# Fifteen instead of eight convolution strips made beside the projections, and a convolution block with wider rings

## Chip, core and metric

One core of one Trainium2 chip runs the whole program as one launch. The metric is the device time of that launch in microseconds, median over runs. PE is TensorE (PEld its weight loads), DVE VectorE, ACT ScalarE, POOL GpSimd, SP SyncE, which only issues transfers and waits here.

## What is computed

One layer of a hybrid decoder, for 528 prompt tokens (16 learned ones and 512 given) and 8 x 4 sample tokens, 560 together. What matters here is the causal convolution of width 4 with SiLU between the input projection and two of the three mixers:

```python
def causal_conv_silu(x, buf, w, b):
    T = x.shape[1]
    xp = jnp.concatenate([buf.astype(x.dtype), x], axis=1)
    y = xp[:, 0:T] * w[0]
    for i in range(1, CONV_W):
        y = y + xp[:, i:i + T] * w[i]
    if b is not None:
        y = y + b
    return jax.nn.silu(y), xp[:, T:]
...
    qa, ka, va, qi, ki, wi, zb, xbc, dtb, qkv, zc, a_raw, b_raw = split_proj(h @ w_in_l)
...
    o_b, ssm_buf, ssm_S = mamba2_mixer(xbc, zb, dtb, ssm_buf, ssm_S, sc_w, sc_b, s_dtb, s_alog, s_d, s_norm, plan)
    o_c, gdn_buf, gdn_S = gdn_mixer(qkv, zc, a_raw, b_raw, gdn_buf, gdn_S, gc_w, g_dtb, g_alog, g_norm, plan)
```

`xbc` (1280 columns) and `qkv` (2304) make 3584 channels: 28 strips of 128. Strips 0 to 5 are x of the Mamba head group, 6 and 7 B, 8 and 9 C, 10 to 27 q, k and v of the DeltaNet group. All but 8 and 9 are needed with tokens on the partitions too. The last three columns of every sequence's raw projection are outputs.

## The kernel before, in words

The program is a row of blocks that follow each other behind a barrier of all engines: three first projections (`pi`), index scores of the samples, the other projections (`pm`), `convolve`, `scans`, tails and gates, prompt attention with the output projection, and the MLP.

**The second projection block** (`project_in`, `pm`) has 52 loads. Loads 0 to 23 (`TOKEN_LOADS`) are token-major; load 24 + f makes strip f, with 128 weight columns and 96 matmuls into two PSUM banks of four. SP brings the weights of a load in two halves, each when DVE (or POOL) has split the half of the load before; ACT makes their high part (`high`, L522), DVE the low part (`low`, L436) from load 43 on. In iteration n ACT copies the two banks of load n out (L553, or L326 for a strip that is convolved here), does `side.scalar`, the high parts of load n+2, and then the convolution's steps. Beside these loads the attention of the samples runs (`side`): POOL gathers rows of cache_v, PE multiplies them with windows that ACT writes (L3070), DVE normalises q and k tiles (L2930) which PE transposes (L3156).

**`ConvAhead`** makes strips 19 to 26 (`AHEAD`) there. `evict` (L326) puts the projection into one of three x buffers, `first_tap` saves the last 35 columns, lays the samples' own columns out (L337, L338) and makes tap 0 with the bias (L342); `taps` are three scalar_tensor_tensor on DVE (L349); `finish` is two SiLU on ACT in place (L360, L362) and a store to the scratch `convT`. SP's queue, ACT's queue and DVE's are all written out by hand: a wait holds up all that is behind it.

**`convolve`** works through 28 positions in the order `STRIPS`. Twenty strips are its own: SP loads a strip from the scratch `projT` into one of R = 4 x buffers (L708), POOL lays out the samples' columns (L734, L735), ACT makes tap 0 (L793), DVE taps 1 to 3 (L867), ACT the SiLU (L749, L752) into `feat` or `bcT`. The eight brought strips are loaded from `convT` (L703) into `feat`, which has four slots: SP waits there for the turning of the strip that held the slot. Each strip but 8 and 9 is turned by four transposes on PE (L893) and a fifth for the last 48 tokens (L894), and ACT copies it to `tm` (L758, L759). The taps' result `y` has two slots. ACT's loop over positions f is: tap 0 of f, SiLU of f-1, copy of f-2, then `gate_steps(f)`.

`gate_steps` puts other work in at fixed positions: the decay gates (Exp at f = 5, Ln at 7, sums on PE at 10, `gate_sums`, L901 to L905, Exp at 12), the squares of q and k for their norm on ACT (L783) and their sums on DVE (L859), five times from `AT_SQUARES` = 14 on, one of a kind waiting for the other since `squares` is one buffer. PE also turns the last columns (`conv_l`, L915) for the state outputs, two strips per position from f = 10, which DVE copies out (L809). The next block's first work is L1021.

Of the kernel before, what the change touches and what calls it, by code (L numbers as in the profile page):

```python
# [16 lines left out]
P = 128  # L17
# [268 lines left out]
AHEAD = range(19, 27)  # L286


class ConvAhead:


    def __init__(self, nc, dram, sb, first_load):
        self.nc, self.dram, self.sb, self.first_load = nc, dram, sb, first_load

    def enter(self, ctx):
        sem = lambda n: ctx.enter_context(self.nc.semaphore(f"ca_{n}"))
        sbuf = lambda n, s: ctx.enter_context(self.nc.sbuf_tensor(f"ca_{n}", s, F32))
        self.x = self.sb["ssc_all"][:, 0:3 * XW].rearrange("p (r w) -> p r w", r=3)
        self.y, self.par, self.state = sbuf("y", [P, 2, YW]), sbuf("par", [P, len(AHEAD), 5]), sbuf("state", [P, len(AHEAD), DB, 3])
        self.par_in, self.zeroed, self.evac, self.laid, self.tapped, self.conv, self.silu = (  # L300
            sem(n) for n in ("par_in", "zeroed", "evac", "laid", "tapped", "conv", "silu"))
        self.chain = sem("chain")
        self.tail_saved = [sem(f"tail_saved{n}") for n in range(3)]
        self.y_saved = [sem(f"y_saved{n}") for n in range(2)]

    def strip(self, n):
        f = n - self.first_load
        return f - AHEAD.start if f in AHEAD else None

    def sync(self, sp):  # L310
        sp.dma_start(self.par[:, :, :], self.dram["conv_par"][:, AHEAD.start:AHEAD.stop, :]).then_inc(self.par_in, 16)
        sp.dma_start(self.state[:, :, :, :], self.dram["conv_state"][:, AHEAD.start:AHEAD.stop]).then_inc(self.par_in, 16)

    def zero(self, dve):
        for r in range(3):
            last = dve.memset(self.x[:, r, 0:3], 0.0)
        last.then_inc(self.zeroed, 1)

    def evict(self, act, a, y, bank, evac):
        if y == 0:  # L320
            if a == 0:
                act.wait_ge(self.zeroed, 1)
            if a >= 3:
                act.wait_ge(self.conv, a - 2)
                act.wait_ge(self.tail_saved[a % 3], 16 * (a // 3))
        act.activation(self.x[:, a % 3, 3 + HALF * y:3 + HALF * (y + 1)], bank[:, 0:HALF], ACT.Copy).then_inc(evac, 1)  # L326

    def first_tap(self, act, a, evac, evicted):
        x = self.x[:, a % 3]
        own = x[:, RAW:XW].rearrange("p (b c) -> p b c", c=7)  # L330
        new = x[:, 3 + TP:RAW].rearrange("p (b c) -> p b c", c=DT)
        rows = slice(R_CONV + P * (AHEAD.start + a), R_CONV + P * (AHEAD.start + a + 1))
        act.wait_ge(evac, evicted)
        act.dma_start(self.dram["projT"][rows, TP - 3:TOK], x[:, TP:RAW]).then_inc(self.tail_saved[a % 3], 16)
        if a == 0:
            act.wait_ge(self.par_in, 32)
        act.activation(own[:, :, 0:3], self.state[:, a], ACT.Copy)  # L337
        act.activation(own[:, :, 3:7], new, ACT.Copy).then_inc(self.laid, 1)  # L338
        act.wait_ge(self.laid, a + 1)
        if a >= 2:  # L340
            act.wait_ge(self.y_saved[a % 2], 16 * (a // 2))
        act.activation(self.y[:, a % 2, :], x[:, 0:YW], ACT.Identity, bias=self.par[:, a, 4:5], scale=self.par[:, a, 0:1]  # L342
                       ).then_inc(self.tapped, 1)
# [12 lines left out]
    def finish(self, act, a):
        y = self.y[:, a % 2, :]
# [3555 lines left out]
```

## Time and profile before

| | |
|---|---|
| runs | 3277.17, 3271.11, 3273.70 us |
| median | 3273.7 us |
| profiled execution | 3272.38 us |
| its span | 3270.6 us |
| busy: PE, DVE, ACT, POOL | 2996.6, 2340.0, 1181.5, 694.0 us |
| mean granted TensorE clock | 0.947 of full speed |
| moved by DMA | 493.29 MB, 151 GB/s |

Busy time is an average over very different stages. PE is busy for 92% of the span, in some slices hardly at all; how the time of a stage comes about has to be read there.

### The profile page before, as it was taken

How to read it: one execution, taken by the hardware profiler on the slowest of the kernel's cores; microseconds unless marked ns; L12 is line 12 of the kernel's file. 1: busy time of each engine (PE TensorE's matmuls, PEld its weight loads, DVE VectorE, ACT ScalarE, POOL GpSimd, SP SyncE). 2: the span in 40 equal slices, each digit the busy share in tenths (PEclk: the TensorE clock that was granted, in tenths of full speed). 3: DMA queues.
4: the chain of work that ended last, by engine and by line, in shares of the span. 5: the costliest groups of instructions: out<-in, count | busy, mean ns of one | idle time of the engine just before them, and what ended most of it. 6: DMA issues, size and time to landing. Idle time of an engine off the chain costs nothing. (4 is left out here: it accounts for less than half of the span.)

```text
span 3270.6 us, 51120 instructions
## 1 busy us (share of the span) xinstructions
PE 2996.6 (92%) x20751; PEld 2750.5 (84%) x20751; DVE 2340.0 (72%) x3028; ACT 1181.5 (36%) x1737; POOL 694.0 (21%) x527
## 2 busy tenths in 40 slices
PE   7978999999996478877898899999999999999998
PEld 6944888999875377864787799999999999999998
DVE  6025994699533666636786688888888888888887
ACT  4223112222443511142332455555555433333332
POOL 5354333467351034232333000000000000000000
PEclk9989999999997589977899899999999999999999
DMA  5423333469683200045533456666666965555552
GB/s 186 116 76 89 90 98 97 137 190 283 192 243 107 65 10 1 1 122 133 157 115 106 146 170 190 190 193 190 187 197 199 318 223 183 187 191 191 196 172 100
DMA packets 499161, 493.29 MB, mean 151 GB/s; under 512 B 33178, under 2 KB 434298, under 8 KB 497541
## 3 DMA queue, kind: packets, MB, share of 16 engines
q1 hardware_dynamic: 463600, 421.81, 42.4%
q0 software_dynamic: 13440, 42.02, 4.1%
q10 hardware_dynamic: 21888, 26.20, 2.3%
q8 instruction: 166, 2.72, 0.3%
q14 instruction: 67, 0.55, 0.1%
HBM read 377.98 MB, written 113.19 MB: 150 GB/s over the span
## 5 line engine op out<-in xcount | busy, mean ns | idle before, releaser
L3684 ACT ACTIVATE om_ring<-om_raw 128x1024 fp32r<-128x1024 f32 x456 | 482.6, 1059 | 598.1 <-PE om_ps L3464 404.8
L3447 PE MATMUL om_ps<-om_hc,om_ring 128*128 128x272 f32 x5376 | 682.4, 290 | 10.1 <-DVE om_ring L3496 6.4
L3447 PEld LDWEIGHTS om_ps<-om_hc,om_ring 128*128 128x128 f32 x5376 | 681.6, 189 | 11.0 <-DVE om_ring L3496 6.8
L3464 PE MATMUL om_ps<-om_hc,om_ring 128*128 128x272 f32 x5376 | 681.8, 290 | 5.8 <-issue 4.6
L3464 PEld LDWEIGHTS om_ps<-om_hc,om_ring 128*128 128x128 f32 x5376 | 680.8, 189 | 6.8 <-issue 5.4
L3496 DVE TENSOR_TENSOR om_ring<-om_raw,om_ring 128x1024 fp32r<-128x1024 f32 x456 | 553.8, 1220 | 129.5 <-ACT om_ring L3684 129.2
L489 PE MATMUL pm_ps<-h,w_ring 128*128 128x280 f32 x2688 | 354.9, 293 | 8.4 <-issue 7.8
L489 PEld LDWEIGHTS pm_ps<-h,w_ring 128*128 128x128 f32 x2688 | 348.7, 189 | 14.3 <-issue 14.3
L436 POOL TENSOR_TENSOR w_ring<-w_raw,w_ring 128x1024 fp32r<-128x1024 f32 (+2 forms) x110 | 251.9, 2310 | 341.6 <-ACT w_ring L522 341.2
L507 PE MATMUL pm_ps<-w_ring,h 128*128 128x512 f32 (+2 forms) x1152 | 237.3, 365 | 8.1 <-POOL w_ring L436 8.1
L507 PEld LDWEIGHTS pm_ps<-w_ring,h 128*128 128x128 f32 x1152 | 199.9, 189 | 42.0 <-issue 8.2
L522 ACT ACTIVATE w_ring<-w_raw 128x1024 fp32r<-128x1024 f32 (+2 forms) x128 | 124.9, 1011 | 275.5 <-PE as_dead_bank L507 176.8
L3614 DVE TENSOR_TENSOR om_x<-om_x,om_ps 128x544 f32<-128x544 f32 x224 | 160.6, 717 | 80.9 <-PE om_ps L3464 78.3
L2123 PE MATMUL ao_w<-ao_mh,ao_ring 128*128 128x272 f32 x1152 | 183.1, 310 | 19.0 <-POOL ao_mh L2263 11.9
L2123 PEld LDWEIGHTS ao_w<-ao_mh,ao_ring 128*128 128x128 f32 x1152 | 158.3, 195 | 35.7 <-issue 18.3
L489 PEld LDWEIGHTS pi_ps<-h,w_ring 128*128 128x128 f32 x768 | 98.5, 188 | 0.1
L489 PE MATMUL pi_ps<-h,w_ring 128*128 128x280 f32 x768 | 98.5, 290 | 0.0
L2998 DVE TENSOR_TENSOR as_prod<-as_rows,as_qb 128x512 f32<-128x512 f32 x64 | 95.7, 1495 | 0.0
L553 ACT ACTIVATE pm_stage<-pm_ps 128x280 f32<-128x280 f32 (+3 forms) x64 | 29.2, 456 | 178.6 <-PE pm_ps L489 132.0
L2537 DVE CAST ss_ptf<-ss_pt_i 128x64 f32<-128x64 int32 x1 | 0.2, 195 | 124.8 <-DMA sm_c_toks<-c_toks 124.8
L2273 POOL TENSOR_TENSOR ao_ring<-ao_raw,ao_ring 128x768 fp32r<-128x768 f32 x32 | 60.8, 1918 | 124.2 <-ACT ao_ring L2207 124.2
L2879 POOL DMA_INDIRECT as_rows<-in_cache_v,as_offs x64 | 66.0, 1032 | 94.9 <-PE as_o_bank L3145 79.9
(563 smaller groups left out, 4041.5 us busy)
## 6 DMA issues: line engine op xcount, KB each, us to landing
om_raw<-in_w_up SPq DMA_DIRECT2D x128, 512.0 KB, 4.9
om_raw<-in_w_down SPq DMA_DIRECT2D x128, 512.0 KB, 5.1
hid_scratch<-om_x SPq DMA_DIRECT2D x64, 952.0 KB, 7.4
om_hc<-hid_scratch SPq DMA_DIRECT2D x56, 1088.0 KB, 11.7
w_raw<-in_w_in SPq DMA_DIRECT2D x112, 512.0 KB, 4.0
ao_raw<-in_w_out SPq DMA_DIRECT2D x32, 384.0 KB, 3.7
as_qb<-q_rows SPq DMA_DIRECT2D x32, 256.0 KB, 4.7
om_x<-xT_scratch SPq DMA_DIRECT2D x7, 1088.0 KB, 11.8
```

What stands on the lines that cost most here:

```text
L436: eng.tensor_tensor(f32r(ring[:, n % 2, 1, half_of(q, n)]), raw[:, q, whole(q, n)], ring[:, n % 2, 0, half_of(q, n)], ALU.subtract).then_i ...
L489: ins = pe.matmul(bank_of(b + y)[:, 0:HALF], piece(a, k), f32r(h[:, x, k, two_halves(y)]), start=first, stop=last)
L507: ins = pe.matmul(bank_of(b + m)[:, 0:w], f32r(h[:, x, ld.k0 + k, tok]), piece(a, k), start=first, stop=last)
L522: act.activation(f32r(ring[:, n % 2, 0, half_of(q, n)]), raw[:, q, whole(q, n)], ACT.Copy).then_inc(hi_ready[q], 1)
L2123: ins = pe.matmul(w_ps[2 * (n % 2) + half][:, 0:HM], w, f32r(mh[:, b, k, kept_half(half)]), start=first, stop=last)
L2879: pool.indirect_dma_start(self.rows[:, n % RING, :], None, table, bass.IndirectOffsetOnAxis(ap=self.offs[:, x, j:j + 1], axis=0)).then_inc ...
L2998: dve.tensor_tensor(prod[:, n % 2, :], self.rows[:, n % RING, :], self.qb[:, j % 4, :], ALU.mult).then_inc(s["multiplied"], 1)
L3447: last = pe.matmul(ps[:, bank_of(q, idx), 0:HM], f32r(ring[:, n % SLOTS, a, P * k:P * (k + 1)]), f32r(hc[:, c, b, k, :]), start=(idx in (0 ...
L3464: last = pe.matmul(ps[:, bank_of(q, idx) + i, 0:HM], w, f32r(hc[:, slot, b, GJ * half + j, :]), start=(idx in (0, 1, 3) and j == a == b == 0),
L3496: dve.tensor_tensor(f32r(ring[:, n % SLOTS, 1, :]), source(n), ring[:, n % SLOTS, 0, :], ALU.subtract).then_inc(lo, 1)
L3614: dve.tensor_tensor(dst, dst, ps[:, b:b + 2, 0:HM], ALU.add).then_inc(gathered, 1)
L3684: act.activation(f32r(ring[:, n % SLOTS, 0, :]), source(n), ACT.Copy).then_inc(hi, 1)
```

## The change

Fifteen strips are made beside the projections: 19 to 26 as before (`DIRECT`), and 10 to 16 (`FETCHED`), which have been projected by then: SP loads them back from `projT`. A direct strip's steps and a fetched strip's stand at the same load, `jobs(n)`. Direct strips have two x buffers instead of three, fetched ones two of their own; the SiLU writes back into the x buffer, from which the store goes, so the `y` slot is free as soon as the SiLU has read it. `finish` of the load before now stands ahead of `first_tap`.

`convolve` has 13 strips of its own, five x buffers, three `y` slots and a buffer `done_ahead` for all fifteen finished strips, loaded in two transfers of eight and seven. SP waits for no turning any more. ACT does the SiLU two positions after tap 0 and the copy after three. The order of strips is another, the squares begin at position 18 and share `done_ahead`'s memory, and the last columns are turned four at a time.

```diff
-AHEAD = range(19, 27)
+FETCHED, DIRECT = tuple(range(10, 17)), tuple(range(19, 27))
+AHEAD = FETCHED + DIRECT
...
+        self.direct, self.fetched = (x[:, 0, :], x[:, 1, :]), (x[:, 2, :], more[:, :])
...
+    def jobs(self, n):
+
+        m, out = n - self.at, []
+        if 0 <= m < len(DIRECT):
+            out.append((m + min(m, len(FETCHED)), len(FETCHED) + m, self.direct[m % 2], m, True))
+        if 0 <= m < len(FETCHED):
+            out.append((2 * m + 1, m, self.fetched[m % 2], m, False))
+        return out
...
+        m = n - 2 - self.at
+        if m == 0:
+            for q in range(4):
+                sp.wait_ge(self.stored[q], 16 * ((self.staged - q + 3) // 4))
+        if 0 <= m < len(FETCHED):
+            if m >= 2:
+                sp.wait_ge(self.fetched_saved[m % 2], 16 * (m // 2))
+            rows = slice(R_CONV + P * FETCHED[m], R_CONV + P * (FETCHED[m] + 1))
+            sp.dma_start(self.fetched[m % 2][:, 3:RAW], self.dram["projT"][rows, :]).then_inc(self.x_in[m % 2], 16)
...
+        act.activation(x[:, 3:3 + TP], y[:, 0:TP], ACT.Silu)
...
-                if strip(n) is not None:
-                    ahead.first_tap(act, strip(n), evac, first_out[n + 1])
-                if n and strip(n - 1) is not None:
-                    ahead.finish(act, strip(n - 1))
+                for job in jobs(n - 1):
+                    ahead.finish(act, job)
+                for job in jobs(n):
+                    ahead.first_tap(act, job, evac, first_out[n + 1])
...
-AT_GATES, AT_SQUARES, L3_AT = 4, 14, 10
-STRIPS = (10, 11, 12, 19, 13, 14, 15, 20, 16, 17, 18, 21, 6, 7, 22, 8, 9, 23, 0, 1, 24, 2, 3, 25, 4, 5, 26, 27)
+AT_GATES, AT_SQUARES, L3_AT = 4, 18, 10
+STRIPS = (17, 10, 18, 11, 0, 12, 13, 1, 14, 15, 2, 16, 19, 20, 21, 3, 22, 4, 23, 5, 24, 6, 25, 7, 26, 8, 9, 27)
...
-        R = 4
-        xp = sbuf("conv_x", [P, R, XW])
-        y = sbuf("conv_y", [P, 2, YW])
+        R, RX, RY = 3, 5, 3
+        xp = sbuf("conv_x", [P, RX, XW])
+        y = sbuf("conv_y", [P, RY, YW])
+        done_ahead = sbuf("conv_ahead", [P, len(AHEAD), TOK])
...
-                if brought(f):
-                    if f >= R:
-                        sp.wait_ge(turned, before(f - R + 1))
-                    sp.dma_start(feat[:, f % R, :], dram["convT"][:, strips[f] - AHEAD.start, :]).then_inc(feat_in[f % R], 16)
...
+            for k, f in enumerate(own_at):
+                if k >= RX:
+                    sp.wait_ge(conv, k - RX + 1)
...
+                if k in (1, 3):
+                    half = slice(AHEAD_HALF * (k > 1), min(len(AHEAD), AHEAD_HALF * (1 + (k > 1))))
+                    sp.dma_start(done_ahead[:, half, :], dram["convT"][:, half, :]).then_inc(ahead_in[k > 1], 16)
...
-            for f in range(NCONV + 2):
+            for f in range(NCONV + 3):
...
-                    if k >= 2:
-                        act.wait_ge(act_ready, k - 1)
+                    if k >= RY:
+                        act.wait_ge(act_ready, k - RY + 1)
...
-                if 1 <= f <= NCONV and not brought(f - 1):
-                    silu(f - 1)
-                if f >= 2 and strips[f - 2] in nth:
-                    tokens_out(f - 2)
+                if 2 <= f <= NCONV + 1 and not brought(f - 2):
+                    silu(f - 2)
+                if f >= 3 and strips[f - 3] in nth:
+                    tokens_out(f - 3)
```

Three places show how instructions move. First ACT in the projection block, one load in the middle of the convolved strips, before (`sm_ssc_all` is where the x buffers lie, `ca_x` the one added, `ca_y` the taps' result):

```order
L326 ACTIVATE sm_ssc_all<-pm_ps 128x280 x2
L3070 ACTIVATE as_win<-as_p_t 128x4 x6
L522 ACTIVATE w_ring<-w_raw 128x1024 x2
L334 DMA projT<-sm_ssc_all 128x35
L337 ACTIVATE sm_ssc_all<-ca_state 128x8x3
L338 ACTIVATE sm_ssc_all<-sm_ssc_all 128x8x4
L342 ACTIVATE ca_y<-sm_ssc_all,ca_par 128x616
L360 ACT_TABLE_LOAD
L360 ACTIVATE ca_y<-ca_y 128x528
L362 ACTIVATE ca_y<-ca_y 128x32
L364 DMA convT_scratch<-ca_y 128x560
```

and the same load's convolution steps now:

```order
L556 ACTIVATE w_ring<-w_raw 128x1024 x2
L392 ACT_TABLE_LOAD
L392 ACTIVATE sm_ssc_all<-ca_y 128x528
L394 ACTIVATE sm_ssc_all<-ca_y 128x32
L396 DMA convT_scratch<-sm_ssc_all 128x560
L392 ACTIVATE sm_ssc_all<-ca_y 128x528
L394 ACTIVATE sm_ssc_all<-ca_y 128x32
L396 DMA convT_scratch<-sm_ssc_all 128x560
L362 DMA projT<-sm_ssc_all 128x35
L370 ACTIVATE ca_y<-sm_ssc_all 128x616
L370 ACTIVATE ca_y<-ca_x,sm_ssc_all 128x616
```

Two finishes and two first taps stand behind the high parts of the weights. Second, SP in the same block now, where the fetch (L338) stands behind the weights and the q and k tile of its load:

```order
L490 DMA w_raw<-in_w_in 128x8x128 x2
L2941 DMA out_k_prompt<-as_qb 128x512
L2956 DMA as_qb<-projN 128x1024
L2961 DMA as_near<-projN 128x64 x2
L338 DMA sm_ssc_all<-projT 128x560
```

Third, SP at the start of `convolve`, before:

```order
L682 DMA conv_par<-in_conv_par 128x140
L683 DMA conv_state<-in_conv_state 128x672
L708 DMA conv_x<-projT 128x560 x3
L703 DMA conv_feat<-convT_scratch 128x560
L689 DMA g_bias<-in_ssm_dt_bias 128x12
```

and now:

```order
L741 DMA conv_x<-projT 128x560
L744 DMA conv_state<-in_conv_state 128x672
L745 DMA conv_par<-in_conv_par 128x140
L741 DMA conv_x<-projT 128x560
L750 DMA conv_ahead<-convT_scratch 128x4480
L741 DMA conv_x<-projT 128x560
L728 DMA g_bias<-in_ssm_dt_bias 128x12
```

Eight finished strips in one transfer stand between the second and the third strip of the block's own.

## Rows read from the trace of the kernel before

**Rows 1.** The page: PE's busy tenths in 40 slices of the span.
```profile
PE   7978999999996478877898899999999999999998
```
**Rows 2.** Busy time by engine in stretches: PE, PEld, DVE, ACT, POOL; clock; DMA share, GB/s.
```profile
940.00:960.00 20.00, 20.00 (x122) 16.33 (x121) 8.65 (x10) 9.06 (x21) 10.74 (x10) 1.00 0.87 257
...
1035.00:1040.00 5.00, 0.00 (x0) 0.00 (x0) 0.66 (x1) 1.41 (x2) 0.71 (x5) 0.50 0.84 282
...
1060.00:1065.00 5.00, 2.18 (x10) 1.70 (x10) 3.16 (x6) 4.23 (x8) 0.13 (x1) 0.80 0.34 107
...
1075.00:1080.00 5.00, 5.00 (x25) 4.72 (x24) 0.00 (x0) 1.55 (x4) 0.00 (x0) 0.50 0.00 0
```
**Rows 3.** Groups by line, 1020 to 1160 us: busy, mean ns, idle before, releaser.
```profile
L867 DVE SCALAR_TENSOR_TENSOR conv_y<-conv_x,conv_par,conv_y 128x616 f32<-128x616 f32 x60 | 51.3, 860 | 40.7 <-ACT conv_y L793 39.2
...
L859 DVE TENSOR_REDUCE rn<-g_squares 128x12 f32<-128x1536 f32 (+1 forms) x5 | 8.7, 1741 | 1.0 <-ACT g_squares L783 1.0
```
**Rows 4.** Waits of SP's queue, 1032 to 1146 us: total, times, longest.
```profile
SPq L703 <- PE conv_small L894: 59.6, 6, 18.8
```
**Rows 5.** Timeline of the block's start: start, duration, engine, line, [idle before].
```profile
1032.88 0.36 SPq L682 DMA_DIRECT2D conv_par<-in_conv_par  x1
...
1038.34 0.90 ACT L793 ACTIVATE conv_y<-conv_x,conv_par 128x616 f32<-128x616 f32 x1 [9.45 <-POOL conv_x L735]
1040.00 0.27 POOL L734 COPY conv_x<-conv_state 128x24 f32<-128x24 f32 x1 [0.54 <-DMA conv_x<-projT]
...
1042.84 0.72 PEld L893 LDWEIGHTS conv_big<-ident,conv_feat 128*128 128x128 f32 x4 [15.85 <-ACT conv_feat L752]
...
1042.89 0.90 ACT L793 ACTIVATE conv_y<-conv_x,conv_par 128x616 f32<-128x616 f32 x1
```
**Rows 6.** Timeline: a SiLU, a turning, its copy, SiLU's table, gate sums and what follows.
```profile
1044.59 0.64 ACT L749 ACTIVATE conv_feat<-conv_y 128x528 f32<-128x528 f32 x1 [0.80 <-DVE conv_y L867]
...
1048.03 0.72 PEld L893 LDWEIGHTS conv_big<-ident,conv_feat 128*128 128x128 f32 x4 [1.76 <-issue]
...
1049.40 0.60 ACT L758 ACTIVATE tm<-conv_big 128x512 f32<-128x512 f32 x1
...
1056.16 1.28 ACT L749 ACT_TABLE_LOAD   x1
...
1073.59 0.55 PEld L901 LDWEIGHTS g_ps<-g,upto 128*128 128x128 f32 x2
...
1080.14 0.17 PEld L915 LDWEIGHTS conv_l<-ident,conv_last 128*27 128x27 f32 x2 [0.34 <-issue]
```
**Rows 7.** Timeline: first square, the fourth of five, the last one, last copy, last norm step.
```profile
1089.63 1.48 ACT L783 ACTIVATE g_squares<-tm 128x1536 f32<-128x1536 f32 x1
...
1107.00 1.48 ACT L783 ACTIVATE g_squares<-tm 128x1536 f32<-128x1536 f32 x1 [1.23 <-DVE rn L859]
...
1113.72 1.48 ACT L783 ACTIVATE g_squares<-tm 48x1536 f32<-48x1536 f32 x1 [4.44 <-DVE rn L859]
...
1142.19 0.26 ACT L759 ACTIVATE tm<-conv_small 48x128 f32<-48x128 f32 x1
...
1144.70 0.18 DVE L878 TENSOR_SCALAR rn<-rn 128x30 f32<-128x30 f32 x1
```
**Rows 8.** Stores of finished strips, 870 to 1010 us: KB, median us to landing.
```profile
convT_scratch<-ca_y ACTq DMA_DIRECT2D x6, 280.0 KB, 6.5
```
**Rows 9.** Timeline of the projections: loads' copies out, values on PE, weights' issue.
```profile
870.55 0.68 ACT L326 ACTIVATE sm_ssc_all<-pm_ps 128x280 f32<-128x280 f32 x2
...
877.47 5.42 PE L3145 MATMUL as_o_bank<-as_rows,as_win 128*128 128x512 f32 x12
...
936.23 0.70 ACT L326 ACTIVATE sm_ssc_all<-pm_ps 128x280 f32<-128x280 f32 x2 [3.29 <-PE pm_ps L489]
...
942.33 1.50 SPq L456 DMA_DIRECT2D w_raw<-in_w_in  x2
...
959.88 0.41 ACT L326 ACTIVATE sm_ssc_all<-pm_ps 128x280 f32<-128x280 f32 x1 [4.24 <-PE pm_ps L489]
```

More of the change, by code:

```diff
@@ L303, in enter @@
[L303 to L312, printed above, removed]
+        old = self.sb["ssc_all"]
@@ new lines, in enter @@
+        x = old[:, 0:3 * XW].rearrange("p (r w) -> p r w", r=3)
+        more = sbuf("x", [P, XW])
+        self.direct, self.fetched = (x[:, 0, :], x[:, 1, :]), (x[:, 2, :], more[:, :])
+        self.par = old[:, 3 * XW:3 * XW + 5 * len(AHEAD)].rearrange("p (f w) -> p f w", w=5)
+        self.y, self.state = sbuf("y", [P, 2, YW]), sbuf("state", [P, len(AHEAD), DB, 3])
+        self.par_in, self.zeroed, self.laid, self.tapped, self.conv, self.silu, self.chain = (
+            sem(n) for n in ("par_in", "zeroed", "laid", "tapped", "conv", "silu", "chain"))
@@ L314, in zero, with evict @@
     def zero(self, dve):
-        for r in range(3):
-            last = dve.memset(self.x[:, r, 0:3], 0.0)
+        for x in (*self.direct, *self.fetched):
+            last = dve.memset(x[:, 0:3], 0.0)
         last.then_inc(self.zeroed, 1)
-    def evict(self, act, a, y, bank, evac):
+    def evict(self, act, m, y, bank, evac):
         if y == 0:
-            if a == 0:
+            if m == 0:
                 act.wait_ge(self.zeroed, 1)
[L323 to L336, printed above, removed]
+            if m >= 2:
+                act.wait_ge(self.tail_saved[m % 2], 16 * (m // 2))
+                act.wait_ge(self.direct_saved[m % 2], 16 * (m // 2))
@@ L337, in first_tap @@
         act.activation(own[:, :, 0:3], self.state[:, a], ACT.Copy)
         act.activation(own[:, :, 3:7], new, ACT.Copy).then_inc(self.laid, 1)
[L339 to L342, printed above, removed]
+        act.wait_ge(self.laid, j + 1)
+        if j >= 2:
+            act.wait_ge(self.silu, j - 1)
+        act.activation(self.y[:, j % 2, :], x[:, 0:YW], ACT.Identity, bias=self.par[:, a, 4:5], scale=self.par[:, a, 0:1]
@@ L461, in _ @@
                     side.sync(sp, n)
-                if ahead and n == TOKEN_LOADS:
-                    ahead.sync(sp)
+                if ahead:
+                    ahead.sync(sp, n)
             if front:
@@ L582, in _ @@
                     ahead.zero(dve)
-                if strip(n - 2) is not None:
-                    ahead.taps(dve, strip(n - 2))
+                for job in jobs(n - 2):
+                    ahead.taps(dve, job)
                 while side and spent < SHARE * n:
                     spent += next(work, SHARE)
-            if strip(N - 2) is not None:
-                ahead.taps(dve, strip(N - 2))
+            for job in jobs(N - 2):
+                ahead.taps(dve, job)
             for _ in work:
@@ L724, in _ @@
             pool.memset(raw[:, :, :], 0.0).then_inc(cleared, 1)
-            for n in range(R):
-                last = pool.memset(xp[:, n, 0:3], 0.0)
-            last.then_inc(zeroed, 1)
+            pool.memset(xp[:, :, 0:3], 0.0).then_inc(zeroed, 1)
             pool.wait_ge(par_in, 32)
```

145 lines of the change are left out of this document (85 added, 60 removed).

## The prediction

> **What bounds the kernel now.** I read PE's busy tenths over the span first [rows 1]: the MLP's slices stand at 9, and where the change works, about 840 to 1145 us, lie a stretch at 9 and one at 3 to 5. The stretches by engine tell them apart. From 940 to 960 us, in the projections, PE is busy for all of 20 us at full clock while DVE and ACT use 8.65 and 9.06 us of the 20 [rows 2]. From 1033 to 1145 us, in `convolve`, no engine is full for long. There the groups by line say who waits: DVE's 60 taps take 51.3 us, and DVE stands idle for 40.7 us before them, nearly all behind ACT's tap 0 [rows 3]; SP stands 59.6 us in front of loads of finished strips, behind PE's turning [rows 4]. The block is a chain that goes from ACT to DVE, to ACT, to PE, to ACT. It runs from SP's first issue at 1032.88 to the end of the last norm step at 1144.88 [rows 5, 7], 112.0 us, and the next block waits for all of it. So work taken out of it shortens the span if the place it goes to has room.
>
> **The projections.** Seven strips are added at loads 19 to 25. Each adds to ACT tap 0 of 0.90 us [rows 5], about 0.4 for laying out and 0.8 for the SiLU pair [rows 6], and to DVE three taps of 0.86, 2.6 us [rows 3]. Two copies out of consecutive loads lie 23.65 us apart (936.23 to 959.88) [rows 9], so per load ACT gets 2.1 us more on some 11 and DVE 2.6 on some 10 of 23.65. In ACT's order they stand behind the weights' high parts, so the weights are not late. I take nothing for them, hidden by PE's matmuls.
>
> What queues behind the new waits: on SP the fetch waits for the store of two fetched strips before. That store is issued a few us after the high parts of the load, lands in 6.5 [rows 8], and SP's next weights go out late in the load in any case (942.33, in the load copied out at 959.88) [rows 9]. The room is about 6 us per load. On ACT, two more steps stand ahead of the windows for PE's values. The tight place is the first: copies out at 870.55, six windows after it, PE's values from 877.47 [rows 9]. If DVE's sum for the q and k tile comes 2.6 us later behind the fetched strip's taps, this copy out slides as much, and some 2 us of room are left. Bounds of this part: nothing (all in the gaps) and +3 us (this place and one more); I take 0, nearest to the idle time of both engines. A gain I exclude, since PE is full there. If the cover went, the seven strips would cost 7 x 4.7 = 33 us.
>
> **The convolution block**, stretch by stretch, with durations from the rows: tap 0 0.9, three taps 2.65, SiLU 0.8 (with its table 2.05, the table being 1.28), turning 1.5 when back to back, copy 0.75, square 1.5 with its sum on DVE 1.75, gate sums 6.5 (1073.59 to 1080.14) [rows 3, 5, 6, 7].
>
> 1. Start to the third own strip's tap 0: before, at 1042.89 [rows 5]. Now its data come behind 3.57 MB: three own strips of 0.287 MB, state and parameters 0.42, and eight finished strips, 2.29. At the 282 GB/s of 1035 to 1040 us [rows 2] that is 12.7 us from the first issue's start of moving, some 1034.5: 1047.2 and, laid out, 1047.4. From 1032.9 this is **14.5 us**, 4.5 more than before.
> 2. To the end of the gate sums: before 1042.9 to 1080.1, 37.2 us. Now ACT: 0.9 + 0.8 + 0.7, a turning and copy 1.4, Exp with table 1.7, so 1052.9; SiLU with table, copy, tap, copy, Ln with table, 6.0, 1058.9; copy, SiLU with table, copy and PE's turning of that strip, 4.1, 1063.0. Then PE alone: two turnings, four last columns 1.05, the sums 6.5, with a small wait 10.6, 1073.6. Together **26.2 us**. Only two of the positions 5 to 10 are own strips, where before it was five.
> 3. To the first square: before 9.5 us. Now Exp with table (2.8 with DVE's sums), two copies 1.9, tap and copy 1.6, turnings at 1.5 with a set of last columns 2.4, tap and SiLU with table 3.0, turning and copy 2.1: **13.8 us**. It is longer since the squares now start four positions later.
> 4. Five squares: before 1089.63 to 1115.20, 25.6 us. A gap without an own strip is 1.5 + 1.8 = 3.3, one with is 6.7 (1107.00 to 1113.72) to 7.3 [rows 7]. Now strips of the block's own stand at two of the four gaps (19 and 21) where it was three: 7.0 + 3.3 + 6.9 + 3.3 + 1.5 = **22.0 us**.
> 5. To the last copy's end: before 1115.2 to 1142.4, 27.2 us, with six own strips to start. Now four. Tap 0.9, taps 2.65, the fifth sum 1.75, a copy of last columns 0.7, then DVE back to back, which three `y` slots allow, 3 x 2.65; SiLU 0.8, turning 1.35, copy 0.75: **17 us**.
> 6. The norm's root and two steps: **2.4 us**, as before [rows 7].
>
> Sum: 14.5 + 26.2 + 13.8 + 22.0 + 17 + 2.4 = 95.9 us, against 112.0: **16.1 us less**. The profiled execution took 3272.4 us, so 3256.3; the median of the runs lies 1.3 above it, 3257.6. I say 3257.
>
> Bounds of the sum: the block's ACT work is 13 x 1.7 + 26 x 0.75 + 5 x 1.5 + gates with tables about 11 = 60 us, with start and end 5.5 + 2.4, 68: nothing below 3230. Above, if no wait goes and only the work of seven strips does not help, 0. Stretch 1 is the one without a row: the trace has no transfer of 2.29 MB. The nearest rows bound its landing, 282 GB/s above, and at 151 GB/s (the whole program's mean) 8 to 10 us more.
>
> The third plain load landed at 1040.00 in the order of issue [rows 5]. The Trainium skill says the same ("DMA: Bandwidth & Descriptors", Queues, rings and completion order): on each DMA engine the descriptors of one issuing queue are consumed in ring order. This speaks against the change: a small, urgent strip behind a large transfer waits for all of it. If the transfers shared the engines evenly instead, stretch 1 would be 10 us and the sum 3253. I take the ordered case, as the trace's landings do.
>
> **Rivals.** *PE's clock comes up in the block.* From 1075 to 1080 PE was busy for 5.00 of 5 us at 0.50 of full speed, its lower level of 1.2 GHz, while 1060 to 1065 was granted 0.80 after less work [rows 2]. In my stretches 2 and 3 PE is busy nearly throughout. At 2.4 GHz the gate sums would take 3.3, and some eight turnings and last columns on the path half: 3.2 + 5 = 8 us less, 3249. Against it: the low level of nearly the whole block before, with PE at under half. The skill's page "TensorE: Matmul & The Clock Gate" (Part 1) says that the throttled state is the default and sustained activity releases it; by that rule this rival would be the case, unless short waits between turnings spoil it. 20%.
>
> *Data late.* The 2.29 MB or the second half behind it, with the last columns in short rows, hold up strips 4 and 5: 8 us more in stretch 1 or 2, 3265. For it: the 0.84 share of the DMA engines at 282 GB/s. 10%.
>
> *Slower: the fetch blocks the weights.* SP waits for a fetched strip's store; if store, fetch and ACT's later steps exceed the room of 6 us and the slack behind it, the weights of the next load come late at each of seven loads. The total reaches the other side from 2.3 us of stall a load (7 x 2.3 = 16); with 4 us a load it is 28 - 16, 3270 to 3286, say 3282. Against it: weights are issued some 17 us ahead of the copy out of their load [rows 9], and DMA share has room outside the bursts. 4%.
>
> *The change does not do what it says*: the seven strips just change place and ACT, waiting for fetches, holds PE for as long as the block gains, 3272. Against it: PE full and ACT half idle. 4%.
>
> **How the numbers follow.** Forecast 62%, with its own range 3252 to 3262. Clock 20%, late data 10%, no net gain 4%, slower 4%. The range takes the forecast, late data up to 3265 and the clock's case down to 3246; left out are the last two and the ends, under 20%. About 0.2%, 6.5 us, is what measurements can tell: over 6.5 faster 91%, within 4%, slower 5%.
>
> **What would show it.** Right: `convolve` lasts 94 to 98 us; tap 0 of the third own strip near 1047; DVE's idle before taps under 20 us; SP no longer waits for turnings; copies out in the projections still 23.6 us apart and the block begins within 3 us of 1033. Wrong: idle time of PE before its weight loads between 850 and 1010 us; gaps between squares above 7 us; granted clock 1.00 in the middle of the block, which would mean the first rival.

## The result and the profile after

| | before | after |
|---|---|---|
| median of 4 runs (us) | 3272.4 (3267.5 to 3277.2) | 3247.3 (3245.7 to 3249.8) |
| ratio to before, 95% interval | | 0.9919 [0.9907, 0.9931] |
| profiled execution, its span | 3272.4, 3270.6 | 3247.4, 3245.5 |
| block `convolve`, first issue to last norm step | 112.0 | 87.3 |

The kernel is 25 us faster; the forecast said 16.7 us faster (3273.7 to 3257). The time lies inside the range of 3246 to 3265, near its low end, and outside the forecast case's own 3252 to 3262.

Of the profiled execution's 25.1 us of span, the block gives 24.7. It begins 1.3 us later, `scans` behind it takes 274.1 us before and 270.1 now, from there to the first load of `w_up` in the MLP it is 439.2 and 439.9, and from that load on 1.5 us more (1.31 - 24.69 - 3.95 + 0.70 + 1.53 = -25.10). The change edits none of the code behind the block. So it is partly luck that block and total agree to 0.4 us. By the forecast's six stretches, with SP's first issue at 1034.19:

| stretch (us) | before | forecast | after |
|---|---|---|---|
| 1. start to third own strip's tap 0 | 10.0 | 14.5 | 12.5 |
| 2. to the end of the gate sums | 37.2 | 26.2 | 22.5 |
| 3. to the first square | 9.5 | 13.8 | 11.8 |
| 4. five squares | 25.6 | 22.0 | 21.6 |
| 5. to the last copy's end | 27.2 | 17 | 16.5 |
| 6. norm | 2.4 | 2.4 | 2.4 |
| block | 112.0 | 95.9 | 87.3 |

The stretches by engine of the kernel after, one in the projections and the others in the block, answer to [rows 2]. Columns are PE, PEld, DVE, ACT, POOL busy; granted clock; DMA share; GB/s.

```profile
940.00:960.00 20.00, 20.00 (x122) 16.19 (x121) 11.19 (x13) 10.96 (x28) 11.36 (x10) 1.00 0.87 262
1035.00:1040.00 5.00, 0.00 (x0) 0.00 (x0) 0.00 (x0) 0.88 (x2) 0.71 (x4) 0.50 0.98 321
1040.00:1045.00 5.00, 1.33 (x5) 0.86 (x5) 4.73 (x6) 1.58 (x4) 0.00 (x0) 0.50 0.95 387
...
1065.00:1070.00 5.00, 5.00 (x38) 4.57 (x37) 1.60 (x5) 2.73 (x6) 0.36 (x2) 0.80 0.21 59
1075.00:1080.00 5.00, 2.18 (x16) 1.87 (x15) 4.89 (x7) 4.24 (x8) 0.47 (x2) 0.82 0.20 57
```

In the projections DVE has 2.5 us more work in these 20 us and ACT 1.9 us more, and PE is as full as before. At the block's start the transfers run at 321 and 387 GB/s, where the forecast had taken 282. The gate sums lie in 1065 to 1070 at 0.80 of full speed; before they ran at 0.50. The clock of a stretch is a mean; the two levels seen are 0.50 (1.2 GHz) and 1.00 (2.4 GHz).

The groups by line, 1020 to 1160 us, answer to [rows 3]:

```profile
L904 DVE SCALAR_TENSOR_TENSOR conv_y<-conv_x,conv_par,conv_y 128x616 f32<-128x616 f32 x39 | 33.3, 859 | 33.5 <-ACT conv_y L830 32.6
...
L896 DVE TENSOR_REDUCE rn<-conv_ahead 128x12 f32<-128x1536 f32 (+1 forms) x5 | 8.7, 1747 | 2.0 <-ACT conv_ahead L820 2.0
L820 ACT ACTIVATE conv_ahead<-tm 128x1536 f32<-128x1536 f32 (+1 forms) x5 | 7.4, 1480 | 8.8 <-DVE rn L896 8.8
```

DVE's taps fell from 60 to 39, 18 us less work. Of its 33.5 us of idle time, 18.7 is the one wait before the block's first tap, so 14.8 are left inside. ACT stands 8.8 us before the squares, behind their sums on DVE. The waits of SP's queue, 1032 to 1125 us, against [rows 4]:

```profile
SPq L741 <- DVE conv_y L904: 25.9, 6, 10.4
```

The 59.6 us behind PE's turning are gone. What SP's loads now wait for is an x buffer, and ahead of need: ACT stands before a tap 0 for its strip only twice, at the first (8.92 us) and at the third (0.94). The timeline of the block, against [rows 5] to [rows 7]:

```profile
1034.19 0.34 SPq L741 DMA_DIRECT2D conv_x<-projT  x1
...
1045.65 1.12 PE L930 MATMUL conv_big<-ident,conv_ahead 128*128 128x128 f32 x4 [0.68 <-DMA conv_ahead<-convT_scratch]
1046.30 0.21 POOL L771 COPY conv_x<-conv_state 128x24 f32<-128x24 f32 x1 [6.55 <-DMA conv_x<-projT]
...
1046.69 0.90 ACT L830 ACTIVATE conv_y<-conv_x,conv_par 128x616 f32<-128x616 f32 x1 [0.94 <-POOL conv_x L772]
...
1051.75 0.21 DVE L855 MEMSET cum<- 128x180 f32 x1 [1.41 <-DMA g_raw<-projN]
...
1052.59 0.28 ACT L804 ACTIVATE g_u<-g_w 128x90 f32<-128x90 f32 x1 [0.58 <-DVE g_w L857]
...
1065.22 0.29 PE L938 MATMUL g_ps<-g,upto 128*128 128x18 f32 x2
...
1067.39 1.28 ACT L811 ACT_TABLE_LOAD   x1
...
1068.29 0.90 PE L942 MATMUL g_el<-g_by_block,ones 48*128 48x162 f32 x2
...
1070.38 0.27 ACT L813 ACTIVATE wend<-wend 128x90 f32<-128x90 f32 x1
...
1080.95 1.47 ACT L820 ACTIVATE conv_ahead<-tm 128x1536 f32<-128x1536 f32 x1
1087.65 1.48 ACT L820 ACTIVATE conv_ahead<-tm 128x1536 f32<-128x1536 f32 x1 [3.15 <-DVE rn L896]
1091.02 1.48 ACT L820 ACTIVATE conv_ahead<-tm 128x1536 f32<-128x1536 f32 x1 [1.24 <-DVE rn L896]
...
1101.09 1.48 ACT L820 ACTIVATE conv_ahead<-tm 48x1536 f32<-48x1536 f32 x1 [1.24 <-DVE rn L896]
...
1118.81 0.26 ACT L796 ACTIVATE tm<-conv_small 48x128 f32<-48x128 f32 x1
...
1121.32 0.18 DVE L915 TENSOR_SCALAR rn<-rn 128x30 f32<-128x30 f32 x1
```

POOL waits 6.55 us for the third own strip, where before it waited 0.54, and PE waits 0.68 us for the first finished strip. DVE and then ACT also wait for the inputs of the gates (`g_raw`), 18.4 us after the block's start. From the first of the gate sums to their end it is 4.0 us, where before it was 6.4. The squares start 6.7, 3.4, 6.7 and 3.4 us apart.

The projections' copies out, against [rows 9]:

```profile
872.00 0.68 ACT L352 ACTIVATE sm_ssc_all<-pm_ps 128x280 f32<-128x280 f32 x2
...
935.52 0.70 ACT L352 ACTIVATE sm_ssc_all<-pm_ps 128x280 f32<-128x280 f32 x2 [1.42 <-PE pm_ps L523]
...
959.17 0.70 ACT L352 ACTIVATE sm_ssc_all<-pm_ps 128x280 f32<-128x280 f32 x2 [3.09 <-PE pm_ps L523]
```

Two of them are 23.65 us apart, as before. The tight place slid by 1.45 us (870.55 to 872.00), inside the 2 us of room.

### The profile page after: what moved, and what is told of

It is laid out like the page before. It is cut to its first block and busy times, and to the rows that moved or that the text cites. A ratio compares the mean times of both kernels' runs of the same rounds, so it can differ in the third digit from the quotient of the medians.

```text
span 3245.5 us, 51124 instructions
## 1 busy us (share of the span) xinstructions
PE 2988.9 (92%) x20751; PEld 2745.5 (85%) x20751; DVE 2343.1 (72%) x3029; ACT 1183.7 (36%) x1751; POOL 695.3 (21%) x510
## 5 line engine op out<-in xcount | busy, mean ns | idle before, releaser
L3485 PEld LDWEIGHTS om_ps<-om_hc,om_ring 128*128 128x128 f32 x5376 | 683.1, 190 | 10.7 <-DVE om_ring L3534 7.0
## 6 DMA issues: line engine op xcount, KB each, us to landing
om_hc<-hid_scratch SPq DMA_DIRECT2D x56, 1088.0 KB, 11.8
om_x<-xT_scratch SPq DMA_DIRECT2D x7, 1088.0 KB, 11.3
```

Source lines behind the costliest of these rows:

```text
L3485: last = pe.matmul(ps[:, bank_of(q, idx), 0:HM], f32r(ring[:, n % SLOTS, a, P * k:P * (k + 1)]), f32r(hc[:, c, b, k, :]), start=(idx in (0 ...
```

## The experiments

One line per kernel, from its profiled execution, in us after the block's first issue, so that a later or earlier start does not mix in. "Gate sums" is where they begin and how long they last, "squares" the five from first start to last end.

| kernel | third tap 0 | gate sums | first square | squares | block |
|---|---|---|---|---|---|
| before | 10.0 | 40.9, 6.4 | 56.8 | 25.6 | 112.0 |
| after | 12.5 | 31.0, 4.0 | 46.8 | 21.6 | 87.3 |
| e0 after again | 12.9 | 31.7, 4.0 | 46.4 | 21.6 | 86.9 |
| e11 after again | 12.8 | 31.6, 3.9 | 46.3 | 21.6 | 86.9 |
| e1 rings only | 10.5 | 42.4, 6.4 | 56.6 | 26.2 | 104.5 |
| e2 strips only | 14.9 | 32.7, 3.9 | 49.8 | 23.8 | 94.5 |
| e5 cover loaded | 11.8 | 30.5, 3.9 | 46.3 | 21.6 | 86.8 |
| e3 two squares | 13.1 | 31.6, 6.4 | 49.1 | 15.0 | 83.0 |
| e10 two squares again | 12.7 | 31.2, 6.4 | 49.4 | 14.9 | 83.2 |
| e4 third strip first | 11.5 | 36.5, 3.9 | 51.9 | 21.6 | 92.4 |
| e8 third, then bulk | 11.3 | 31.6, 6.4 | 49.2 | 21.6 | 89.8 |
| e9 e3 and e8 | 11.5 | 31.4, 6.4 | 49.0 | 14.9 | 82.8 |
| e6 PE kept busy | 16.4 | 32.7, 3.5 | 46.5 | 21.7 | 86.5 |
| e7 e3, e4 and e6 | 17.4 | 37.7, 3.5 | 51.1 | 14.9 | 86.9 |

### How firm the result is

The kernel after, unedited, once alone and once in the last group of kernels.

> The changed kernel once more, unaltered, for a second profile of it. The first profile has the gate sums on PE in 4.0 us at a granted clock of 0.80, where 6.5 was forecast at 0.50. If the clock's place in the block belongs to the kernel (PE is fed there without a gap), the gate sums again take 3.3 to 4.5 us and the block 86 to 89 us. Rival, the clock comes by chance: gate sums near 6.5 us and the block up to 3 us longer.

> The changed kernel unedited, as the partner of the three others of this call: ratio to the kernel before 0.990 to 0.993 as first measured, block 86.5 to 88 us.

e0 took 3253.7 us, e11 3245.8 (ratio 0.9907 [0.9889, 0.9925]). The block agrees to 0.4 us, with gate sums of 4.0 and 3.9 us, as expected. Most of e0's extra 6 us lie between the end of `scans` and the MLP's load of `w_up` (446 against 440 us), in code that no kernel here changes. `scans` itself, unchanged too, lasts from 269.3 to 278.7 us over all the profiled executions here. So the block's length is the sharper measure of an edit, and a difference of some us between two kernels' times is not to be read without it. The block's start, too, moves by itself: the eleven profiled executions with the new projections unedited begin it between 1031.3 and 1034.9, with 1032.9 before and 1033.6 in e1 (the old eight strips) among them.

### The two halves of the change

Rings only: the new block with five x buffers, three `y` slots and one buffer for the finished strips, but eight strips made ahead and the old order.

```diff
-FETCHED, DIRECT = tuple(range(10, 17)), tuple(range(19, 27))
+FETCHED, DIRECT = (), tuple(range(19, 27))
...
-AT_GATES, AT_SQUARES, L3_AT = 4, 18, 10
+AT_GATES, AT_SQUARES, L3_AT = 4, 15, 10
```

> The new convolution block (five x buffers, three y slots, a buffer for finished strips, SiLU after two positions, last columns by fours) with the old eight strips made ahead and the old order of strips. Theory (both halves are needed): block of 98 to 104 us against 112.0 before and 87.3 after, whole kernel 9 to 14 us faster than before. Rival A (the rings and SP's missing wait are all of it): block under 92 us, 20 to 25 us faster. Rival B (only the strips taken out count): block over 108 us, within 4 us of before. The projections end as before, block start 1033.

It took 3269.8 us, ratio 0.9985 [0.9976, 0.9994]; block 104.5, so 7.5 us less. Both miss what was expected, the block barely and the time clearly: of the 7.5 us the median shows 3.5, and the profiled execution none, since its `scans` lasted 278.7 us against 274.1. Strips only: fifteen made ahead and the new order, in the old block with its four `feat` slots as the landing place.

```diff
-        R, RX, RY = 3, 5, 3
+        R = 4
...
-AT_GATES, AT_SQUARES, L3_AT = 4, 18, 10
+AT_GATES, AT_SQUARES, L3_AT = 4, 17, 10
```

> Fifteen strips ahead, with the old block (four x buffers, two y slots, one load per finished strip behind the turning of its slot), the new order of strips, and squares from position 17. Theory: block of 98 to 106 us, 6 to 14 us faster than before, SP waiting for turnings over 40 us. Rival A: block over 108 us. Rival B: block under 92 us. The block starts near 1034, 1.3 us later than before, as in the changed kernel.

3254.5 us, ratio 0.9943 [0.9928, 0.9958]; block 94.5, so 17.5 us less, more than the 6 to 14 that were expected. The two add up to 25.0, against 24.7 for both, but two things make this less neat than it looks. The gate sums ran slow in e1 and before (6.4 us) and fast in e2 and after (3.9), so 2.5 of e2's 17.5 us are the clock's. And the rings gain in other places: alone behind the squares, on top of the strips (94.5 to 87.3) 3.0 us up to the first square, 2.2 in the squares and 2.0 behind them. SP's waits show what each lacks (first fence rings only, second strips only):

```profile
SPq L741 <- DVE conv_y L904: 59.3, 12, 10.3
```

```profile
SPq L737 <- PE conv_small L928: 46.0, 12, 11.4
```

With rings alone SP's loads wait only for x buffers, and the gain comes at the end: behind the fifth square the block takes 21.8 us instead of 29.7, but gate sums and squares are as late as before. With strips alone the gate sums begin 8 us earlier, and SP still stands 46 us behind PE's turnings; its third own strip starts at 14.9 us, later than with the rings. The strips, with the order that goes with them, carry about two thirds of the gain. The seven strips' 18 us of DVE work is near its size; that DVE's work is what sets it was not tested, and strips and order were not taken apart.

### What covers the seven strips

Each fetched strip gets two more tap 0 on ACT and three more passes on DVE beside the projections; the values stay what they are.

```diff
+        for r in range(0 if direct else 3):
+            dve.tensor_tensor(y, y, y, ALU.max).then_inc(self.again, 1)
...
+        for r in range(0 if direct else 2):
+            act.activation(self.y[:, j % 2, :], x[:, 0:YW], ACT.Identity, bias=self.par[:, a, 4:5], scale=self.par[:, a, 0:1]).then_inc(self.again_act, 1)
```

> The changed kernel with more work for each fetched strip beside the projections: two more tap 0 on ACT (1.8 us) and three more passes on DVE (2.6 us), results as before. Theory (this work lies beside full PE with room): block start stays at 1034 within 1.5 us, and the time within 3 us of the changed kernel's 3247. Rival (the cover is used up): each of seven loads gets 1.8 to 2.6 us longer, 13 to 18 us in all.

3246.9 us, ratio 0.9922 [0.9903, 0.994], the same as the change itself, as the theory had it. The block's start does not keep to the theory: 1036.2, not within 1.5 us of 1034. The stretch 850 to 1010 us, first the kernel after, then this one:

```profile
850.00:1010.00 160.00, 157.08 (x893) 122.64 (x892) 75.60 (x90) 79.64 (x201) 64.39 (x56) 0.99 0.69 213
```

```profile
850.00:1010.00 160.00, 155.90 (x890) 121.95 (x888) 92.68 (x111) 87.81 (x209) 65.89 (x56) 0.99 0.70 210
```

DVE has 17.1 us more to do in these 160 and ACT 8.2 (12.6 us of new tap 0, with other work moved past the window's end), and PE is busy for 1.2 less. The block begins 2.0 us later than in the kernel after, 1.2 later than in the latest of its unedited repeats, and the total does not show it. So the projections take in nearly twice the 4.7 us per strip for 2 to 3 us, where the rival had 13 to 18, and the change's own strips are hidden.

### The squares

Two buffers of squares in place of one, both in `done_ahead`'s memory:

```diff
-        squares = done_ahead[:, 0:3, :].rearrange(...)
+        squares = [done_ahead[:, 3 * b:3 * b + 3, :].rearrange(...) for b in range(2)]
...
-                    if i:
-                        act.wait_ge(summed, i)
+                    if i >= 2:
+                        act.wait_ge(summed, i - 1)
```

> The changed kernel with two buffers for the squares instead of one (both in the finished strips' memory). Theory (in the squares' stretch ACT and DVE take turns on the one buffer): from the first square to the end of the last 15 to 17 us instead of 21.6, block 81 to 83 us instead of 87.3, 4 to 6 us faster than the changed kernel. Rival (DVE's own work is the limit there, or the saving is lost behind it in the last own strips): block 86 to 87.5 us.

3240.8 us, ratio 0.9899 [0.9884, 0.9914]. Its groups by line:

```profile
L897 DVE TENSOR_REDUCE rn<-conv_ahead 128x12 f32<-128x1536 f32 (+1 forms) x5 | 8.7, 1738 | 0.0
L821 ACT ACTIVATE conv_ahead<-tm 128x1536 f32<-128x1536 f32 (+1 forms) x5 | 7.4, 1479 | 2.3 <-DVE rn L897 2.3
```

ACT's wait before the squares falls from 8.8 to 2.3 us and the five take 15.0 instead of 21.6. The block gains 4.3 although its gate sums happened to run slow (6.4 us), which costs 2.5. Again, beside the kernel after on the same chip:

> The kernel with two buffers of squares again, beside the changed kernel on one chip. If its gain over the changed kernel is real: ratio to the kernel before 0.988 to 0.991, at least 4 us under the changed kernel's. Rival, it was chance: within 2 us of it.

3242.9 us (0.9891 [0.9873, 0.9908]) against 3245.8; block 83.2 against 86.9. The block's gain is repeated; in time it is 3.0 us, under the 4 that were expected, and the intervals overlap. What the second buffer is worth is seen best between e8 and e9 below, which differ by this edit alone and both have slow gate sums: block 89.8 and 82.8, so 7.0 us.

### The third strip behind the large transfer

First attempt: the third own strip, and then the finished strips.

```diff
-                if k in (1, 3):
+                if k in (2, 3):
```

> The changed kernel with the first eight finished strips issued behind the third own strip instead of ahead of it. Theory (transfers of SP's queue land in the order of issue): tap 0 of the third own strip 6 to 8 us after the block's start instead of 12.5; but ACT's next step needs a finished strip, so the gate sums end at most 1 to 2 us sooner. Rival (the transfers share the engines evenly): tap 0 of the third moves by under 2 us. Rival 2 (this lateness was the whole of stretch 1's price): block 4 us or more shorter.

3251.4 us, ratio 0.9933 [0.9918, 0.9948], and the block 5 us longer. The edit did more than its name says: at k = 2 the gate inputs are issued first, 18 small transfers, so the large one went out at 1042.81, 10.8 us after the block's start. The third strip itself was laid out 6.5 us after the start, but its tap 0 moved only from 12.5 to 11.5 us, not to the 6 to 8 that were expected. PE pays:

```profile
1050.81 1.12 PE L930 MATMUL conv_big<-ident,conv_ahead 128*128 128x128 f32 x4 [8.06 <-DMA conv_ahead<-convT_scratch]
```

Second attempt, with the gate inputs behind both:

```diff
+                if k in (2, 3):
+                    half = slice(AHEAD_HALF * (k > 2), min(len(AHEAD), AHEAD_HALF * (1 + (k > 2))))
+                    sp.dma_start(done_ahead[:, half, :], dram["convT"][:, half, :]).then_inc(ahead_in[k > 2], 16)
                 if k == 2:
                     gate_inputs()
-                if k in (1, 3):
```

> The third own strip is issued ahead of the eight finished strips, and the small gate inputs stay behind both (in the kernel with the third strip first of an earlier run, they stood between). If ring order alone made the third own strip late, its tap 0 is ready to start some 2 us sooner after the block's first issue (near 11 instead of 12.5 us), while the finished strips land about 0.8 us later than now, with PE waiting 1.5 instead of 0.7 us for them; block 85.5 to 87.5 us, time 3245 to 3249. Rival, the large transfer must be first because PE has nothing else to turn: the block is then 88 us or more.

3245.1 us, ratio 0.9909 [0.9889, 0.9928], level with the kernel after. Its block's start:

```profile
1037.59 0.90 ACT L830 ACTIVATE conv_y<-conv_x,conv_par 128x616 f32<-128x616 f32 x1 [8.80 <-POOL conv_x L772]
...
1039.05 0.48 POOL L771 COPY conv_x<-conv_state 128x24 f32<-128x24 f32 x1 [0.33 <-DMA conv_x<-projT]
...
1044.12 0.89 ACT L830 ACTIVATE conv_y<-conv_x,conv_par 128x616 f32<-128x616 f32 x1
...
1044.91 1.11 PE L930 MATMUL conv_big<-ident,conv_ahead 128*128 128x128 f32 x4 [1.48 <-DMA conv_ahead<-convT_scratch]
```

The third strip is laid out from 1039.05, 6.3 us after the start, where behind the large transfer it was 12.1 (after) and 12.4 (e11): the landing follows the order of issue. Tap 0 moves only from 12.8 to 11.3, since ACT's own order then holds it, and the gate sums begin at 31.6 us in this kernel and in e11. So this part of the third strip's delay, 1.5 us, is not on the path at all. The trace says what is:

```profile
1050.38 0.21 DVE L855 MEMSET cum<- 128x180 f32 x1 [2.61 <-DMA g_raw<-projN]
...
1051.20 0.28 ACT L804 ACTIVATE g_u<-g_w 128x90 f32<-128x90 f32 x1 [1.57 <-DVE g_w L857]
```

DVE waits for the last of the gates' 18 small inputs, and the Exp that needs them starts 18.4 us after the block's start here, and 18.4 in the kernel after, e0 and e11 as well. What ACT gains by the earlier strip it stands idle for there, 1.57 us instead of 0.26 in e11. No run moved these inputs alone.

The block of e8 is 2.9 us longer than e11's; 2.5 of that are the gate sums, at 6.4 instead of 3.9. By the letter that is the rival's "88 us or more", but not for its reason: with gate sums of 3.9 the block would be 87.3, and PE waits 1.48 us, as expected.

> Both edits, third strip ahead of the large transfer and two buffers of squares. If they act on different stretches, the block is the two-squares kernel's 83.0 us less what the order alone gives or costs: 81.5 to 83.5, time 3239 to 3242. Rival, the front's gain is absorbed by the gate sums' wait: 83, no difference from two squares.

3236.6 us, ratio 0.9881 [0.9863, 0.9899], the fastest of all kernels here and below the 3239 to 3242 that were expected: 9.2 us under e11 in the same group. The block explains 4.1 of it (82.8 against 86.9), and against e10, the same kernel without the reordering, only 0.4. Of the 8.1 us between the profiled executions of e9 and e10, 3.1 are an earlier start and 4.7 lie between `scans`' first matmul and the MLP's first load. Against e8, the same kernel without the second buffer, the block gives 7.0 of 8.5 us. The time was seen; that the reordering earns any of it was not shown.

### The clock

Matmuls of the identity with itself, whose results nobody reads, fill PE's gaps at eight places of the block:

```diff
+            WARM = {1: 60, 5: 18, 8: 12, 16: 10, 20: 32, 22: 32, 28: 32, 29: 18}
...
+                for n in range(WARM.get(f, 0)):
+                    pe.matmul(warm_ps, ident[:, :], ident[:, :], start=n == 0, stop=n == WARM[f] - 1)
```

> The changed kernel with matmuls that nobody reads at eight places of PE's order in the convolution block where it stood idle for 2 to 14 us, so that its clock may come up. Theory (the low clock costs only where PE is on the chain): granted clock 0.9 or more over most of the block, turnings 0.8 instead of 1.5 us, block 3 to 6 us shorter than 87.3. Rival (PE is hidden, the clock worth nothing here): within 1 us of 87.3. Where the matmuls outlast the idle time, it costs them.

3254.4 us, ratio 0.994 [0.9924, 0.9955]; block 86.5. Its stretches, and the first filling:

```profile
1040.00:1045.00 5.00, 5.00 (x47) 5.00 (x46) 4.46 (x6) 1.84 (x4) 0.02 (x1) 1.00 0.95 391
...
1065.00:1070.00 5.00, 4.77 (x44) 4.36 (x42) 3.98 (x12) 3.01 (x9) 0.36 (x2) 1.00 0.01 3
...
1080.00:1100.00 20.00, 16.05 (x143) 15.27 (x142) 13.14 (x14) 12.15 (x22) 1.22 (x6) 1.00 0.11 29
```

```profile
1034.63 15.16 PE L950 MATMUL g_ps<-ident 128*128 128x128 f32 x120 [4.57 <-PEq L2485]
```

The block is 0.8 us shorter than after, which by what was expected is the rival's case. At full clock the gate sums take 3.5 us, and from the third tap 0 to the first square it is 30.1 us instead of 34.3. But the first filling lasts until 1049.8, in front of the first turning, and pushes the third tap 0 to 16.4, which gives 3.9 of the 4.2 back. Squares and what follows last what they did (40.0 against 40.5 us), so there PE's clock is off the path. The slower total comes from elsewhere: 717.6 us from `scans`' first matmul to the MLP's load of `w_up`, against 710.0. The unedited e0 had 718.1 there, so this is no proof against the filling, though e7 with the same filling has 719.7; why, stays open.

> All three together: two buffers for squares, the third own strip ahead of the finished ones, and matmuls that nobody reads to keep PE's clock up. If the savings lie on the chain one after the other, block 74 to 79 us, 8 to 13 us faster than the changed kernel; if they cover each other, no better than the best of the three alone.

3256.6 us, ratio 0.9945 [0.9931, 0.9958]; block 86.9, not the 74 to 79 of savings that add up. It carries e4's misplaced gate inputs and e6's long filling, and two squares win back the difference; it settles nothing that the others don't.

## Why the prediction was right and wrong

**Right: where the time goes.** The block's chain bounds this part, work taken out of it shortens the span, and the projections have room. The copies out stay 23.65 us apart, PE's busy time from 850 to 1010 us is 157.08 us in both profiles, and the block begins 1.3 us later, of bounds of 0 to 3, which is less than its start moves between executions; e5 shows that this room was not nearly used up. SP's wait for turnings is gone. One sign failed as it was worded: DVE's idle time before taps is 33.5 us, not under 20; the sign had left out the 18.7 us ahead of the block's first tap, and 14.8 are left without it. Stretches 4, 5 and 6 came out within 0.5 us each; the gaps of 6.7 with an own strip and 3.4 without are near the forecast's 7.0 and 6.9, and 3.3, and e3 shows that the one buffer makes them.

**Wrong: the size, in stretches 1 to 3.** The mechanism held; what failed is the price of single terms of the sum, and one wait that it left out. Stretches 1 to 3 are 7.7 us of the 8.6 by which the block was overestimated; the other 0.9 lies in 4 and 5. Of the 7.7, 2.5 are the clock in the gate sums, which may be chance (see the rival of the clock); 5.2 are the forecast's own.

Stretch 1, 2.0 us: "282 GB/s of 1035 to 1040 us" was taken for the landing. With the large transfer under way the kernel after moved 321 and 387 GB/s; with single strips only, before had 282 and e2 274 in the same 5 us. The ordering itself held. What failed besides is that the third strip's landing was a term of the path and the gates' inputs were none: e8 moves the third tap 0 by 1.5 us and the gate sums not at all, since ACT then waits for those inputs.

Stretch 2, 3.7 us: 2.5 are the gate sums, priced at 6.5 from a row at half clock and run at 0.80. The steps ahead of them took 18.5 us where 19.7 had been added up. In there ACT's first steps, up to the second SiLU's table, were 0.8 too cheap, the next ones 0.3 too dear, and "PE alone: two turnings, four last columns 1.05" with its small wait was 1.7 too dear, 4.1 against 2.4 (1062.83 to 1065.22). In e10, where the clock was 0.50 over the same steps, they took 3.0 us; so 0.6 is the clock, which came up early in the kernel after, and 1.1 is the price of 1.5 for a turning "when back to back". Before, the turnings behind the gate sums start 1.5 us apart, but a pair of last columns stands between them; two without one are 1.1 apart. The first three lines are of before, the last two of after:

```profile
1080.56 1.06 PE L893 MATMUL conv_big<-ident,conv_feat 128*128 128x128 f32 x4
...
1081.63 0.63 PE L915 MATMUL conv_l<-ident,conv_last 128*27 128x128 f32 x2
1082.06 1.06 PE L893 MATMUL conv_big<-ident,conv_feat 128*128 128x128 f32 x4
```

```profile
1056.30 1.06 PE L930 MATMUL conv_big<-ident,conv_ahead 128*128 128x128 f32 x4
...
1057.36 1.09 PE L930 MATMUL conv_big<-ident,conv_ahead 128*128 128x128 f32 x4
```

So the last columns were counted twice, in the turning's price and by themselves.

Stretch 3, 2.0 us: "Exp with table (2.8 with DVE's sums)" was 1.3 too dear. The table is loaded at 1067.39, beside the gate sums, and from their end to that of ACT's last Exp it is 1.5 us (1069.19 to 1070.65). "Turnings at 1.5 with a set of last columns 2.4" was 1.0 too dear, 1.4 measured, by the same double count and with the clock up for its last part. The two copies were 0.6 too cheap, as ACT waits for PE there, and the rest adds 0.3.

The clock has a part in stretch 3 as well. By the mean granted clock of the stretch it lasts 11.8 us at 0.65 in the kernel after, 11.2 at 0.78 in e8, 10.7 at 0.84 in e0 and e11, and 10.3 at 1.00 in e6; e4, with 11.5 at 0.80, is the one a little off this line. The whole range is 1.4 us.

**The rival of the clock** was given 20% and 8 us. Its sign was seen (1.00 from 1065.22 to 1067.72 in the kernel after), its size was not. The gate sums' 2.5 us are real and reach the block's end (e8 against e11), but they are not safely the change's: 3.9 to 4.0 us in after, e0, e2, e4, e5 and e11, 6.4 in before, e1, e3, e8, e9 and e10, and an edit behind the gate sums (e3) is enough to find them slow. With 6.4 the block would be some 89.8, and the time some 2.5 us above what was measured, still below the forecast. Where PE was kept busy, in e6, the clock stood at 1.00 in every stretch read from 1040 us on, which agrees with the Trainium skill ("TensorE: Matmul & The Clock Gate", Part 1: throttled by default, released by sustained activity); but all of it brought 4.2 us at most between third tap and first square, not 8.

**The rival by ring order** fell on the side that was taken. The forecast used the Trainium skill's rule ("DMA: Bandwidth & Descriptors", Queues, rings and completion order); e8 agrees with it, 6.3 against 12.1 us for one strip before or behind 2.29 MB. That it "speaks against the change" by 4.5 us was too much: 2.5 more than before were seen, and 1.5 of them cost nothing.

**Data late, slower, no net gain** did not happen. PE's only wait for finished strips is 0.68 us.

What stays open: how much earlier the gate sums would start with their inputs issued sooner but behind the finished strips; what decides the clock's level in them; and what moves `scans` and the time between `scans` and the MLP by some us from one execution to the next.

## What to carry to other kernels

Work from a stretch bound by waits can go beside one where a single engine is full, and the room is measured by loading the cover until it shows, not by its idle share alone. When a path is added up step by step, ask of each price what else stood in the row that it was read from, and of each step whether the next really waits for it: here a turning's price held the last columns that were then added again, a table load that ran beside the gate sums was put behind them, and the inputs that ACT in fact waits for were not in the sum. One scratch buffer between two engines costs a full round trip per use, and a second one, in memory that was already free, brought 7.0 us in the block with the gate sums at one speed (e8, e9), and 3.7 to 4.3 where they ran slower than in the partner. So compare two kernels only after looking whether the clock treated them alike.

## What was not expected of the hardware

The same gate sums run in 3.9 to 4.0 or in 6.4 us, and PE's busy share ahead of them does not tell which. Four stretches in a row, the last two those of the sums, first of e11 and then of e10, columns as above:

```profile
1059.63:1062.13 2.50, 1.58 (x8) 1.56 (x9) 2.40 (x13) 2.45 (x6) 1.50 (x8) 0.50 0.71 264
1062.13:1064.63 2.50, 2.50 (x14) 2.20 (x13) 2.40 (x3) 1.25 (x4) 0.89 (x2) 0.50 0.00 0
1064.63:1067.13 2.50, 2.50 (x21) 2.50 (x20) 0.00 (x0) 2.42 (x5) 0.00 (x0) 0.81 0.43 118
1067.13:1069.63 2.50, 2.50 (x20) 2.13 (x20) 0.98 (x4) 0.56 (x3) 0.36 (x2) 0.87 0.00 0
```

```profile
1060.62:1063.12 2.50, 1.58 (x8) 1.56 (x9) 2.28 (x13) 2.45 (x6) 1.29 (x7) 0.50 0.68 258
1063.12:1065.62 2.50, 2.50 (x14) 2.20 (x13) 2.40 (x3) 1.25 (x4) 0.87 (x2) 0.50 0.00 0
1065.62:1068.12 2.50, 2.50 (x14) 2.50 (x13) 0.00 (x0) 2.42 (x5) 0.00 (x0) 0.50 0.36 118
1068.12:1070.62 2.50, 2.50 (x13) 2.50 (x12) 0.00 (x0) 0.27 (x1) 0.36 (x2) 0.50 0.00 0
```

PE is busy for the same shares of the four stretches in both, and before the sums the granted clock is 0.50 in both; then it rises to 0.81 and 0.87 in the one and stays in the other. The Trainium skill ("TensorE: Matmul & The Clock Gate", Part 1) says that the point at which the clock rises differs from run to run of one kernel. Three profiles of the kernel after agree: in 2.5 us stretches from the start of the gate sums on it has 1.00 and 0.55 in the first, 0.81 and 0.87 in e11, 0.80 and 0.88 in e0. The time of the sums itself repeated from profile to profile of one program (fast in three of the kernel after, slow in two of two squares), though two squares differs only in steps behind the gate sums. It moves the block by 2.5 us, as much as nearly twice the load on the cover cost.
